# Ending a mixture-of-experts block with tokens on partitions: the last expert's rows summed in PSUM, the norm taken by rows

## The reference

```
h = modulate(rms_norm(x, g_ffn), sh2, sc2)                # 512 tokens x 1024
gates, experts = softmax(top_4(h @ w_router + b_router))  # 4 of 32 experts per token
for each expert e and each of its tokens:
    y[token] += gate * (swiglu(h[token] @ w_in[e] + b_in[e]) @ w_out[e] + b_out[e])
x = x + gt2 * y                                           # gt2: 1024 values from the condition
out = x * rsqrt(mean(x * x, axis=-1) + 1e-6) * g_final    # norm over the 1024 columns of each token
```

## Time and profile before

| | |
|---|---|
| median of 3 executions | 4145.77 us (4142.92 to 4148.1) |
| the profiled execution, its own time | 4145.19 us |
| its span, first to last instruction | 4143.4 us |
| PE, DVE, ACT, POOL busy | 92%, 57%, 41%, 3% of the span |
| granted TensorE clock, mean | 0.959 of 2.4 GHz |

### The profile page before, as it was taken

One profiled execution on the slowest core, in us unless ns is written; L12 is line 12 of the kernel. 1 busy time (PEld: TensorE's weight loads), 2 busy tenths in 40 slices (PEclk: granted clock), 3 DMA queues, 4 the chain that ended last, 5 costly groups with the idle time before them and its releaser, 6 DMA issues.

```text
span 4143.4 us, 75110 instructions
## 1 busy us (share of the span) xinstructions
PE 3832.5 (92%) x32155; PEld 2896.8 (70%) x32155; DVE 2362.8 (57%) x2780; ACT 1694.3 (41%) x2084; POOL 122.4 (3%) x144
## 2 busy tenths in 40 slices
PE   7987988999999987998999899987999999999996
PEld 5866874788877765784787577445777777777774
DVE  5965653422232865663433344644777777777774
ACT  3246652100021355652101243533665666566653
POOL 0000000000000000000000000000000000000000
PEclk9998999999999997999999999997999999999998
DMA  5430002111122440002222312204899999999994
GB/s 226 154 151 3 4 4 83 51 61 63 68 79 77 183 153 32 4 4 92 92 92 82 141 61 92 72 21 183 307 343 353 350 341 349 353 351 342 348 352 167
DMA packets 114079, 650.96 MB, mean 157 GB/s; under 512 B 15008, under 2 KB 15008, under 8 KB 56096
## 3 DMA queue, kind: packets, MB, share of 16 engines
q1 hardware_dynamic: 101344, 610.54, 39.2%
q0 software_dynamic: 12464, 36.38, 3.3%
HBM read 637.35 MB, written 27.46 MB: 160 GB/s over the span
## 4 chain that ended last, share of the span: by engine, by line
PE 84%; DVE 7%; ACT 5%; issue 2%; DMA 1%; SPq 0%; DVEq 0%; POOL 0%; POOLq 0%; ACTq 0%
PE psum L867 51%; PE psum L1651 17%; PE psum L1677 5%; PE psum L1668 4%; PE psum L1062 2%; DVE work L1832 1%; PE psum L1644 1%; PE psum L1635 1%; ACT work L2828 1%; PE psum L1625 1%; PE psum L1504 1%; DVE work L2393 1%; ACT work L2832 1%; DMA ring<-stream 0%; DVE ring_parts L1885 0%
## 5 line engine op out<-in xcount | busy, mean ns | idle before, releaser
L867 PE MATMUL psum<-ht_parts,ahead_parts 128*128 128x512 f32 (+1 forms) x2032 | 689.0, 356 | 3.0 <-DVE ht_parts L1800 2.3
L867 PE MATMUL psum<-work_parts,ring_parts 128*128 128x512 f32 (+1 forms) x1504 | 540.2, 360 | 0.0
L867 PE MATMUL psum<-work_parts,ahead_parts 128*128 128x512 f32 (+1 forms) x1408 | 494.8, 362 | 17.7 <-ACT work_parts L2679 15.6
L867 PEld LDWEIGHTS psum<-ht_parts,ahead_parts 128*128 128x128 f32 (+1 forms) x2032 | 377.0, 188 | 66.8 <-DVE ht_parts L1800 4.0
L867 PE MATMUL psum<-work 64*64 64x64 f32 (+3 forms) x9494 | 369.9, 247 | 55.3 <-ACT work L2832 27.9
L867 PEld LDWEIGHTS psum<-work 64*64 64x64 f32 (+2 forms) x9494 | 273.6, 140 | 141.6 <-issue 96.0
L867 PEld LDWEIGHTS psum<-work_parts,ring_parts 128*128 128x128 f32 x1504 | 285.9, 190 | 46.5 <-issue 1.7
L867 PEld LDWEIGHTS psum<-work_parts,ahead_parts 128*128 128x128 f32 x1408 | 265.9, 190 | 63.3 <-issue 21.8
L1651 PE MATMUL psum<-work_parts 128*128 128x512 f32 x1024 | 273.6, 394 | 0.1
L2518 DVE TENSOR_TENSOR ring_parts<-ring,work_parts 128x2048 fp32r<-128x2048 f32 x97 | 221.9, 2288 | 74.6 <-ACT work_parts L3162 74.6
L2926 ACT ACTIVATE work<-psum 128x512 f32<-128x512 f32 x44 | 26.3, 598 | 547.2 <-PE psum L867 547.2
(11 more groups left out here) (362 smaller groups left out, 6630.2 us busy)
## 6 DMA issues: line engine op xcount, KB each, us to landing
ring<-stream SPq DMA_DIRECT2D x192, 1024.0 KB, 4.8
ring<-w_in SPq DMA_DIRECT2D x192, 1024.0 KB, 6.8
ht<-w_in SPq DMA_DIRECT2D x64, 1024.0 KB, 6.1
ht<-w_out SPq DMA_DIRECT2D x64, 1024.0 KB, 7.3
ring<-w_out SPq DMA_DIRECT2D x64, 1024.0 KB, 7.0
xt<-x_wide SPq DMA_DIRECT2D x8, 391.5 KB, 14.9
xt<-x_wide POOLq DMA_DIRECT2D x1, 3132.0 KB, 10.5
xt_rows<-xt POOLq DMA_DIRECT2D x8, 391.5 KB, 2.7
```

Source lines behind the costliest of these rows:

```text
L867: mm = pe.matmul(*args, **kwargs)
```

## The change

- **Two rows spread over the partitions.** Before the router, ACT makes 16 diagonal tiles of 128 by 128: the identity scaled by `gt2` (eight) and by `g_final` (eight). In `routing`, after the last `turn_rows`, PE multiplies the all-ones matrix by them (two places of 8 products); ACT copies the two results to `gate_row` and `final_row` in the dead columns of `xt`, ahead of `top_exp`. Each holds, on every partition, 1024 values along the free axis.
- **The last expert's rows are not scattered.** Expert 31 of round 0 gets no `gated_rows` on ACT, no `scatter`. DVE's `last_rows` makes four one-hot tiles (`place_hot`: which of the 128 rows goes to which of the 128 tokens of a tile) and, once the last output product is done, one instruction `y_last` = PSUM times gate times `gate_row`.
- **The sums are read earlier.** POOL waits for the scatter of expert 30 and reads the four tiles at once, ahead of its flag and branch, with a semaphore for each tile.
- **The end by rows.** DVE multiplies each tile by `gate_row`. PE forms in PSUM, for each tile, the residual turned to rows (8 products of a block of `xt` with the identity) plus `place_hot` times `y_last` (two products of 512 columns). DVE adds both (`summed`); ACT squares with a running sum and takes a square root; DVE takes the reciprocal and multiplies by it and by `final_row` (`normed_rows`); SP stores the tile. The mean over the partitions, the logarithm and the exponential, and the second transposes are gone.

The core of the diff (new names of tiles left out where a line only places them in memory):

```diff
+        gate_row, final_row = cs(xt[:, 0:4, :]), cs(xt[:, 4:8, :])
+        y_last = con2[:, C2OFF["cos"][0]:C2OFF["cos"][0] + DM]
+        place_hot = rs[:, 0:SEQ]
...
@@ sync
             for t in range(TQ):
-                sp.wait_ge(fin_row_act if t % 2 else fin_row, t // 2 + 1)
+                sp.wait_ge(fin_row, t + 1)
                 sp.dma_start(out[0, P * t:P * t + P, :], out_buf[:, t, :]).then_inc(stored, 16)
@@ gpsimd
                 scatter(r * NE + NE - 2)
-                scatter(r * NE + NE - 1)
-                pool.wait_ge(scattered, 16 * (r + 1) * NE)
+                if r:
+                    scatter(r * NE + NE - 1)
+                pool.wait_ge(scattered, 16 * ((r + 1) * NE - 1))
...
             experts(0)
+            read_sums()
             pool.wait_ge(rank_ready, 1)
             over = pool.alloc_register("over_pool")
...
-            for t in range(TQ):
-                pool.dma_start(y_tok[:, t, :], sum_rows[P * t:P * t + P, :]).then_inc(sums_in, 16)
@@ tensor, routing
                 for t in range(1, TQ):
                     turn_rows(t)
+                pe.wait_ge(rows_spread, 1)
+                for i in range(2):
+                    j, stands, n_stands = banks.place("act")
+                    if stands:
+                        pe.wait_ge(freed[stands], n_stands)
+                    for k in range(KT):
+                        mm = matmul(psum[:, 2 * j + k // 4, P * (k % 4):P * (k % 4) + P], C2("ones"), diag[:, i, k, :], start=True, stop=True)
+                    mm.then_inc(ready["act"], 1)
@@ tensor, the end (after the branch)
-            (32 transposes of y_tok, 8 products with mean_dm, 32 transposes of xt)
+            for t in range(TQ):
+                if t == TQ - 1:
+                    pe.wait_ge(y_ready, NE)
+                for k in range(KT):
+                    pe.matmul(psum[:, 2 * t + k // 4, P * (k % 4):P * (k % 4) + P], xt[:, k, XO + P * t:XO + P * t + P], ident,
+                              start=(k % 4 == 0), stop=False)
+                if t == 0:
+                    pe.wait_ge(y_ready, NE)
+                for c in range(2):
+                    mm = pe.matmul(psum[:, 2 * t + c, :], place_hot[:, P * t:P * t + P], y_last[:, 512 * c:512 * c + 512], start=False, stop=True)
+                mm.then_inc(fin_sum, 1)
@@ vector
+            def last_rows():
+                for t in range(TQ):
+                    ts(last_ids[:, t:t + 1], table[:, 0, NE - 1, 0:1].bitcast(U32), float(-P * t), None, ALU.add).then_inc(dve_chain, 1)
+                dve.wait_ge(dve_chain, w.next(dve_chain, TQ))
+                for t in range(TQ):
+                    ts(place_hot[:, P * t:P * t + P], iota_row, last_ids[:, t:t + 1], None, ALU.is_equal)
+                dve.wait_ge(out_done, NE)
+                stt(in_rows(y_last), psum[:, 6:8, :].rearrange("p b (k c) -> p (b k) c", c=CTX), table[:, 0, NE - 1, 1:2], gate_row, ALU.mult, ALU.mult
+                    ).then_inc(y_ready, 1)
...
                 act_low_part()
-                expert_gate(r, NE - 1)
+                if r:
+                    expert_gate(r, NE - 1)
+                else:
+                    last_rows()
@@ vector, the end (after the branch)
-            (8 scalar_tensor_tensor into xt, 8 more for the norm, 2 copies out of PSUM)
+            def summed(t):
+                dve.wait_ge(fin_sum, t + 1)
+                tt(y_tok[:, t, :], psum[:, 2 * t:2 * t + 2, :].rearrange("p b c -> p (b c)"), y_tok[:, t, :], ALU.add).then_inc(fin_chain, 1)
+
+            def normed_rows(t):
+                dve.wait_ge(fin_std, 2 * t + 2)
+                dve.reciprocal(fin_dev[:, t:t + 1], fin_dev[:, t:t + 1]).then_inc(fin_inv, 1)
+                dve.wait_ge(fin_inv, t + 1)
+                stt(in_rows(out_buf[:, t, :]), in_rows(y_tok[:, t, :]), fin_dev[:, t:t + 1], final_row, ALU.mult, ALU.mult).then_inc(fin_row, 1)
+
+            for t in range(TQ):
+                dve.wait_ge(sums_in[t], 16)
+                tt(in_rows(y_tok[:, t, :]), in_rows(y_tok[:, t, :]), gate_row, ALU.mult).then_inc(fin_chain, 1)
+            dve.wait_ge(fin_chain, TQ)
+            (summed 0, summed 1, normed 0, summed 2, normed 1, summed 3, normed 2, normed 3)
@@ scalar, routing
+                for row in (gate_row, final_row):
+                    j = banks.pair("act")
+                    act.wait_ge(ready["act"], banks.n["act"])
+                    fn(row, psum[:, 2 * j:2 * j + 2, :].rearrange("p b (k c) -> p (b k) c", c=CTX), ACT.Copy).then_inc(freed["act"], 1)
                 act.wait_ge(top_ready, w.next(top_ready))
                 fn(expv, expv, ACT.Exp).then_inc(top_exp, 1)
@@ scalar, after the attention
+            act.wait_ge(modulated, w.next(modulated))
+            for k in range(KT):
+                fn(diag[:, 0, k, :], ident, ACT.Identity, scale=mod[0][:, 5, k, 0:1])
+                ins = fn(diag[:, 1, k, :], ident, ACT.Identity, scale=V("final2", k))
+            ins.then_inc(rows_spread, 1)
@@ scalar, the end (after the branch)
-            (8 squares, Ln, Exp, 2 copies out of PSUM)
+            fn(junk, junk, ACT.Sqrt, bias=EPS, scale=0.0)
+            for t in range(TQ):
+                act.wait_ge(fin_chain, TQ + t + 1)
+                fn(sig, y_tok[:, t, :], ACT.Square, accum_out=fin_ms[:, t:t + 1]).then_inc(fin_std, 1)
+                act.wait_ge(fin_std, 2 * t + 1)
+                fn(fin_dev[:, t:t + 1], fin_ms[:, t:t + 1], ACT.Sqrt, bias=EPS, scale=1.0 / DM).then_inc(fin_std, 1)
```

More of the change, by code:

```diff
@@ L316, in build, with xs, cs @@
         rec = work[:, zoff:zoff + 21 * 512 + 64]
+        def xs(t):
+            return t[..., XO:XO + SEQ]
+        def cs(t):
+            return t[..., 0:CTX]
         def wide(i, n=1):
@@ L362, in carve_parts @@
             return carve(n), work_parts[:, at[0] - n:at[0]]
+        diag = work[:, at[0]:at[0] + 2 * DM].rearrange("p (i k c) -> p i k c", i=2, k=KT)
         x_high, x_low = (carve_parts(DM)[1].rearrange("p (k c) -> p k c", k=KT) for _ in range(2))
@@ L512, in build @@
         scattered = sem("scattered")
-        sums_in = sem("sums_in")
+        sums_in = [sem(f"sums_in{t}") for t in range(TQ)]
+        rows_spread = sem("rows_spread")
         fin_sum = sem("fin_sum")
@@ L824, in scatter @@
                 if n:
-                    pool.wait_ge(scattered, 16 * n)
+                    pool.wait_ge(scattered, 16 * (n - int(n >= NE)))
                 else:
@@ L841, in experts, with read_sums @@
                 scatter(r * NE + NE - 2)
-                scatter(r * NE + NE - 1)
-                pool.wait_ge(scattered, 16 * (r + 1) * NE)
+                if r:
+                    scatter(r * NE + NE - 1)
+                pool.wait_ge(scattered, 16 * ((r + 1) * NE - 1))
+            def read_sums():
+                for t in range(TQ):
+                    pool.dma_start(y_tok[:, t, :], sum_rows[P * t:P * t + P, :]).then_inc(sums_in[t], 16)
             experts(0)
+            read_sums()
             pool.wait_ge(rank_ready, 1)
@@ L852, in _ @@
                     experts(r)
-            for t in range(TQ):
-                pool.dma_start(y_tok[:, t, :], sum_rows[P * t:P * t + P, :]).then_inc(sums_in, 16)
+                for t in range(TQ):
+                    pool.wait_ge(sums_in[t], 16)
+                read_sums()
         @block.tensor
@@ L1725, in _ @@
                     experts(r)
[L1726 to L1729, removed]
-                mm.then_inc(fin_sum, 1)
[L1732 to L1741, removed]
+                pe.wait_ge(y_ready, ROUNDS * NE)
+            for t in range(TQ):
[8 more added lines that the diff above has]
+                    mm = pe.matmul(psum[:, 2 * t + c, :], place_hot[:, P * t:P * t + P], y_last[:, 512 * c:512 * c + 512], start=False, stop=True)
+                mm.then_inc(fin_sum, 1)
         @block.vector
@@ L2428, in routing @@
                 dve.wait_ge(freed["dve"], banks.n["dve"])
-                for _ in range(TQ - 1):
+                for _ in range(TQ - 1 + 2):
                     banks.pair("act")
@@ L2606, in _ @@
                     experts(r)
[L2609 to L2619, removed]
+                for t in range(TQ):
+                    dve.wait_ge(sums_in[t], 32)
+            def summed(t):
[6 more added lines that the diff above has]
+                stt(in_rows(out_buf[:, t, :]), in_rows(y_tok[:, t, :]), fin_dev[:, t:t + 1], final_row, ALU.mult, ALU.mult).then_inc(fin_row, 1)
+            for t in range(TQ):
+                dve.wait_ge(sums_in[t], 16)
+                tt(in_rows(y_tok[:, t, :]), in_rows(y_tok[:, t, :]), gate_row, ALU.mult).then_inc(fin_chain, 1)
+            dve.wait_ge(fin_chain, TQ)
+            summed(0)
+            summed(1)
+            normed_rows(0)
+            summed(2)
+            normed_rows(1)
+            summed(3)
+            normed_rows(2)
+            normed_rows(3)
         @block.scalar
@@ L3218, in experts @@
                 act_high_part()
-                gated_rows()
```

(4 more changed lines are left out.)

14 lines of the change are left out of this document (5 added, 9 removed).

## The result

The changed kernel takes 4119.12 us (median of 4 executions, 4111.84 to 4124.87) against 4144.35 (4 executions, 4141.92 to 4148.1): ratio 0.9937, 95% interval 0.9919 to 0.9956. Timed again beside the last experiment it is 4114.39 (6 executions) against 4142.99 (11): 0.9934, 0.9919 to 0.9949. It is faster, by 25 and by 29 us where 24 were predicted.

A forecast was written before the change was run, and what follows sets the result against it. It took the serial chain behind the last output product, 49.9 us in which nothing streams, as what to cut. 4143.4 - 24.9 + 0.6 = 4119.1 of span, 4120.9 own time, 4121.5 us beside the median; range 4114 to 4129.

The forecast's parts named there:

- The tail: From the last output product's end to the end of the span: 49.9 us before, predicted 24.9 less.
- The branch: DVE's flag and branch after the row of expert 31: bounds 0 and 3.55 us, 3.55 taken.
- The store: Only the last store open at the end: 0.1, landing 3.9, then 0.4, in all 4.4 us; bounds 3 and 5.9.
- PE not the end: At the end DVE, not PE, sets the time, tile 3 ahead by 1.3 us; DVE 0.58, rival PE 0.2.
- lower bound of 4118: Forecast time in us if neither DVE nor PE pays for the branch at the end.
- The rival with PE's branch and a fallen clock: At the end PE starts at 4097, its first 4 us at 1.2 GHz: 4125.8 us; PE sets the end, chance 0.2.
- Sums early: POOL's reads put the last tile at about 4093, DVE comes after 4094.7: no cost, cover 2 to 5 us.
- tables: Rival at the end: ACT changes tables in every tile, two loads of 1.28 us each; time 4129.7, chance 0.04.
- expert loop: Rival: PE's 28 backward branches wait for code, up to 2.98 us each, time 4205; slower, chance 0.03.
- ACT's diagonals: Ahead of the router: 16 diagonals cost some 5, at most 10 us, within 11.17 us of ACT's idle time; nothing lost.
- The router: Exponential 1.9 us late for DVE, eating 1.8 of slack, 0.6 left with gaps; 3.2 at half clock.
- The router doesn't warm up: Clock expected to fall among the ranks; rival: it holds, experts start 10 us earlier, 4111.5; fully or partly, chance 0.12.

The follow-up runs named there:

- a2: The changed kernel once more, unedited, timed beside the version with five edits: 4114.39 us, median of 6, ratio to before 0.9934.
- x2: Changed kernel with logarithm and exponential per tile in place of square root and reciprocal: 4137.3 us.
- x3: Changed kernel with ACT's exponential of the router's picks ahead of the two copies of spread rows: 4113.6 us.
- x7: Changed kernel with the sixteen bias-row records over all 128 partitions instead of 32: 4115.3 us.
- x4: Changed kernel with DVE's last part written first, in the branch side that is fallen into, not jumped to: 4130.7 us.
- x5: Last experiment, on the changed kernel: exponential first, bias rows over 128 partitions, DVE's branch not jumped, early gate-row and identity products: 4106.82 us, ratio to before 0.9908.

## Why the prediction held, and where its steps were off

**The tail: 27.7 us less, 24.9 predicted.** From T0, by the prediction's own steps:

| step | predicted | after |
|---|---|---|
| `last_rows`, branch, to the first product with the gate row | 4.7 | 3.73 |
| four products | 5.0 | 4.66 |
| two sums | 2.4 | 2.36 |
| the rest to the last `normed_rows` | 8.5 | 8.39 |
| last store to the end | 4.4 | 3.06 |
| tail | 25.0 | 22.2 |

The mechanism was right; two terms were too large. The branch was priced whole, 3.55 behind the end of the row of expert 31. In after DVE's register load (0.54) and branch ran while that row was still being made, so that only 2.4 of the stall of 3.06 showed as idle time. The stall itself was near POOL's 2.98; in the four other executions with this jump on DVE's path (a2, x2, x3, x7) it was 2.81 to 2.88. x4, which takes the jump away, removes it. The Trainium skill (Runtime: NRT & Kernel Launch, Instruction fetch mechanics) says that a taken branch whose target isn't among the fetched pages stalls until a DMA has brought the page; the trace agrees on DVE, where one packet of instructions moves in the 3.06 us. PE takes the same branch and shows none of it: its residual products start 0.1 ahead of T0. The prediction's reason holds, its sequencer ran ahead: the register load stands at 4080.5 and the branch at 4081.1, under the last output product. The store was priced by four that left nearly together (3.9 to landing); in after the rows get ready 1.5 to 2.5 us apart, a store lands in 2.7 at the median, and from the end of the last row to the end of the span it is 3.06:

```profile
out_dram<-work SPq DMA_DIRECT2D x4, 512.0 KB, 2.7
```

The total fits in part by luck. The median of 4119.12 lies 2.4 from the forecast, while single executions of after lie 13 apart; by segments the tail gained 2.8 more than predicted, the router lost 0.8 more, and the experts' 0.6 was not forecast.

**PE not the end: right, by about 1 us (1.3 predicted).** PE runs without pause from T0 in after as in x4, where its last tile stands at T0+14.1; DVE comes to that tile at 4102.88 in after, T0+15.1. With DVE's branch gone (x4) PE was the end. So the prediction's lower bound of 4118, with no branch on DVE, did not follow from its own layout: PE's last tile stood only 1.3 ahead, and no more than that could be gained. x4 gained 0.8 at DVE's last row. The rival with PE's branch and a fallen clock did not occur: PE never stopped, and the clock is 1.00 from 4078 to 4102.

```profile
4078.00:4102.00 24.00, 23.89 (x110) 15.31 (x108) 11.33 (x12) 3.07 (x7) 2.25 (x4) 1.00 0.28 104
```

**Sums early, tables, expert loop: right.** The reads left 8.9 us ahead of T0 (8.5 predicted), and nothing waits for them. One table load. ACT's diagonals took 4.8 us, and 4.83 of its idle time was left ahead of the first residual tile:

```profile
2750.33 0.39 ACT L3281 ACTIVATE work<-con,vec 128x128 f32<-128x128 f32 x1
2755.55 0.63 ACT L2693 ACTIVATE work<-xt 128x512 f32<-128x512 f32 x1 [4.83 <-DVEq L2192]
```

The experts took 1232.4 against 1233.0, so no turn got longer.

**The router: +0.6 predicted, +1.4 measured.** DVE's wait for the exponential was sized at 1.9 and measured 1.67. The step that failed is what was counted as slack: 1.8 us of DVE's idle time between the picks and the copy that releases the bias rows. DVE took the exponential 1.68 later than before, counted from the mean square, and the bias rows still started 1.41 later: 0.27 was eaten, not 1.8. Before, PE's 28 rank records ran through this time beside DVE; after, the first 20 are done early, but the last eight need the bank pair that DVE frees with its first rank product, so they now stand behind DVE (1.91 at half clock) instead of beside it. x3 shows both parts: with the exponential first the wait is gone, the eight records run at full clock, and the router is 1.0 below before.

**The router doesn't warm up: right, for another reason.** The prediction expected the clock to fall among the ranks; it fell in a new pause of 2.68 us. But x3 closes most of that pause and the bias rows still run at 0.50, while x7 keeps the pause and they rise to 1.00. What kept the stretch at 1.2 GHz, then, was not the pause: with the bias rows over 128 partitions, and nothing else changed, the clock returned to 2.4 GHz during the first eight of them. The id products go over 128 partitions in every version, and in after they passed 7.1 us at 0.50, so no rule on partitions follows from it.

What stays open is why the unchanged part ahead of the router takes up to 19 us more or less from one profiled execution to the next; of the two first profiles, after is 2.6 us late at 1336 us and 6.9 early at 1874 (POOL's transfers there), and 6.4 early at the router. No run here was made for it.

## What to carry to other kernels

Read the end of a kernel as a list of what each engine waits for in order, and price a change by laying out the new list from the last event that the change can't move; two parts of such a serial end come out near their sum, as 17.4 and 10.1 did, but list for each version which branches and products lie on its path, or one of them is counted twice. Before calling an engine's idle time slack, look whether another engine's work stands in it because of a shared buffer. And when one engine is relieved, look who is next: here 2.5 us taken from DVE were worth 0.8 at its last row and 0.2 at the end of the span until PE was relieved too.

## What the runs showed of the hardware

- Through 21.3 us of unbroken work the granted clock stayed at 0.50 (before, after, x3): sixteen records of 512 columns over 32 of 128 partitions, 14.4 us, and between them 32 of 64 columns over 128 partitions, 7.1 us. With zeros in the other 96 partitions, so that the sixteen go over 128, it went from 0.50 to 1.00 during the first eight (x7, x5).
- Behind a taken branch stood 2.98 us without a wait on POOL (before) and 2.81 to 3.06 on DVE (after, a2, x2, x3, x7), with one packet of instructions moving in it (before, after). On PE nothing shows: its branch stands 6.7 us ahead of T0, under the last output product. Where DVE falls through (x4), its next instruction follows the one ahead of the branch with no gap: it starts 1.20 us behind the start of one of 1.28 us.
- The same store of 512 KB landed in 3.9 us at the median when four left within 1.7 us (before), and in 2.7 when they left 1.5 to 2.5 us apart (after).
- The load behind the bias rows took 5.8 us in after, and 8.7 and 9.9 in x7 and x5 with the same bytes, where POOL's four writes fall closer to it. That the writes hold it up was not tested.
